# HGRN decays kept as factors and multiplied in place, level by level, and RWKV's normalisation taken by token halves

## The reference

```python
def rwkv7_time_mix(...):                       # B, its end: 8 heads of 64
    mean = jnp.mean(o, axis=-1, keepdims=True)
    var = jnp.mean(jnp.square(o - mean), axis=-1, keepdims=True)
    o = ((o - mean) * lax.rsqrt(var + RWKV_LN_EPS)).reshape(B, S, W_B)
    o = o * ln_w + ln_b
    o = o + bonus.reshape(B, S, W_B)
    return o * g

def hgrn2_mix(p, lower_bound, norm_w):         # C: 4 heads, 128 keys, 128 values
    q, fz, i, g = jnp.split(p, 4, axis=-1)
    q = jax.nn.silu(q).reshape(B, S, H_C, DK_C)
    log_f = jnp.logaddexp(jnp.log(lb), jnp.log1p(-lb) + jax.nn.log_sigmoid(fz))
    k = -jnp.expm1(log_f)                      # k = 1 - f
    o = hgrn2_chunked(q, k, i, log_f)          # S_t = f_t * S_(t-1) + k_t v_t ;  o_t = q_t S_t
    return rms_norm_2(o, norm_w) * jax.nn.silu(g)
```

## Time and profile before

| | us |
|---|---|
| median of 3 runs | 3694.24 (3691.92 to 3695.18) |
| the profiled execution | 3689.92 |
| its span | 3688.1 |
| PE busy | 3578.8 (97%) |
| DVE busy | 2229.6 (60%) |
| ACT busy | 1547.7 (42%) |

### The profile page before, as it was taken

One profiled execution on the slowest core, in us unless ns is written; L12 is line 12 of the kernel. 1 busy time (PEld: TensorE's weight loads), 2 busy tenths in 40 slices (PEclk: granted clock), 3 DMA queues, 4 the chain that ended last, 5 costly groups with the idle time before them and its releaser, 6 DMA issues.

```text
span 3688.1 us, 49956 instructions
## 1 busy us (share of the span) xinstructions
PE 3578.8 (97%) x19351; PEld 2892.5 (78%) x19351; DVE 2229.6 (60%) x2501; ACT 1547.7 (42%) x2051; POOL 1059.6 (29%) x567
## 2 busy tenths in 40 slices
PE   8999999999999999999999999998999999998999
PEld 7887888887888778888778786776788786776787
DVE  5666767567666357666666545547555545447654
ACT  4365444454344354444644432224444432324443
POOL 6800838404848018383057000011000001011000
PEclk9999999999999999999999999999999999998999
DMA  8745767556767257675466454312465553312563
GB/s 267 246 133 182 246 212 247 185 155 219 254 202 237 96 178 262 206 251 178 141 229 230 153 187 118 119 59 81 159 206 193 169 168 105 137 36 101 175 203 125
DMA packets 494426, 649.95 MB, mean 176 GB/s; under 512 B 17227, under 2 KB 394594, under 8 KB 494242
## 3 DMA queue, kind: packets, MB, share of 16 engines
q1 hardware_dynamic: 473508, 569.62, 46.8%
q0 software_dynamic: 19584, 75.50, 5.8%
q10 hardware_dynamic: 1150, 2.29, 0.2%
HBM read 646.29 MB, written 1.05 MB: 176 GB/s over the span
## 4 chain that ended last, share of the span: by engine, by line
issue 57%; POOLq 20%; PE 13%; POOL 7%; ACT 0%; DMA 0%; DVE 0%; SPq 0%; ACTq 0%; DVEq 0%
POOLq L642 8%; POOLq L644 6%; POOLq L646 6%; PE bank L1526 4%; PE bank L994 3%; POOL mod_zone L649 3%; POOL modrow L649 2%; PE bank L964 1%; POOL modrow L631 1%; POOL mod_zone L631 1%; PE bank L971 1%; PE bank L973 1%; PE bank L972 1%; POOL rstd L608 1%; PE bank L1723 0%
## 5 line engine op out<-in xcount | busy, mean ns | idle before, releaser
L2596 DVE TENSOR_TENSOR wproj_lo<-wproj,wproj_hi 128x2048 fp32r<-128x2048 f32 x252 | 757.4, 3010 | 129.4 <-ACT wproj_hi L1989 129.4
L994 PE MATMUL bank<-wproj_lo,x_hi 128*128 128x512 f32 x2112 | 538.4, 397 | 0.6 <-ACT x_hi L1980 0.6
L994 PE MATMUL bank<-wproj_hi,x_hi 128*128 128x512 f32 x2112 | 531.0, 393 | 6.6 <-DVE arena L2717 2.8
L994 PE MATMUL bank<-wproj_hi,x_lo 128*128 128x512 f32 x2112 | 523.6, 390 | 0.6 <-DVE x_lo L2657 0.6
L2038 ACT CAST actT_hi<-bank 128x512 fp32r<-128x512 f32 x132 | 77.5, 587 | 1051.1 <-PE bank L1022 1051.1
L994 PEld LDWEIGHTS bank<-wproj_hi,x_hi 128*128 128x128 f32 x2112 | 396.6, 189 | 96.9 <-issue 7.3
L1989 ACT CAST wproj_hi<-wproj 128x2048 fp32r<-128x2048 f32 x252 | 470.5, 1913 | 4.8 <-DMA wproj<-in_ffn_w_gate_up 4.6
L994 PEld LDWEIGHTS bank<-wproj_hi,x_lo 128*128 128x128 f32 x2112 | 396.6, 188 | 83.0 <-DVE x_lo L2657 1.1
L606 POOL TENSOR_SCALAR rstd<-sumsq 128x1 f32<-128x1 f32 x38 | 7.2, 190 | 1546.6 <-ACT tok L1961 1546.3
L994 PEld LDWEIGHTS bank<-wproj_lo,x_hi 128*128 128x128 f32 x2112 | 388.1, 189 | 79.3 <-ACT x_hi L1980 3.3
L2727 DVE TENSOR_TENSOR actT_lo<-bank,actT_hi 128x512 fp32r<-128x512 f32 x132 | 91.2, 691 | 566.0 <-ACT actT_hi L2038 566.0
(11 more groups left out here) (451 smaller groups left out, 5259.6 us busy)
## 6 DMA issues: line engine op xcount, KB each, us to landing
wproj<-in_ffn_w_gate_up SPq DMA_DIRECT2D x336, 512.0 KB, 6.2
wdown<-in_ffn_w_down SPq DMA_DIRECT2D x132, 1024.0 KB, 4.9
wproj<-in_ffn_w_gate SPq DMA_DIRECT2D x84, 512.0 KB, 5.0
wproj<-in_ffn_w_up SPq DMA_DIRECT2D x84, 512.0 KB, 6.2
wproj<-in_w_in SPq DMA_DIRECT2D x40, 1024.0 KB, 7.2
mod_zone<-in_mod_w POOLq DMA_DIRECT2D x36, 1024.0 KB, 6.4
modrow<-in_mod_w POOLq DMA_DIRECT2D x36, 1024.0 KB, 6.0
wproj<-in_sb_w_qkv SPq DMA_DIRECT2D x96, 256.0 KB, 4.3
```

Of the source, the lines that this page charges most:

```text
L994: last = nc.tensor.matmul(proj_ps[t][:, :], rounded(x_part[of_x](c)[:, toks]), rounded(w_part[of_w][:, c, :]), start=start and c == 0, sto ...
L2596: V.tensor_tensor(rounded(wproj_lo[w.odd][:, cols]), src[:, cols], wproj_hi[w.odd][:, cols], ALU.subtract).then_inc(cols_lo, 1)
```

## The change

**Factors for logarithms.** As soon as ACT has copied the first half of RWKV's outputs (`oc0`), it computes `hf` = sigmoid(fz), `hk` = sigmoid(-fz), `hq` = silu(q) and `h_g` = silu(g); `hgrn` on ACT no longer takes a part in the levels. DVE (`decays`) applies the lower bound in the second layer (two operations for each of 4 chunks, as before, but on the factors), and makes `decayed` = hq * hf. At each level DVE (`lengthen(m)`) multiplies the second halves of `decayed` by the product over their block's first half, and the first halves of `hk` by the product over the second, both in place, and makes the products of the next level in `h_total` (512, 256, ... 16 elements, none at m = 64). PE reads `hk` and `decayed` themselves. Since they are changed in place, DVE waits before each level until PE has finished the scores of the level before.

**RWKV's normalisation** up to `ln_ss` is done for each token half by itself, the first while ACT waits for the second. PE's `turn` moves from ahead of HGRN's first scores to behind values(1), and `finish_rwkv` is cut in three steps, one behind each of the levels 1, 2 and 3. ACT's casts (`xg_hi`, `o_hi`, blocks 1 and 2) are no longer spread over the levels but stand one behind the other.

The core of the diff:

```diff
 # PE, hgrn(l)
-                pe.wait_ge(*rw_v.at(l, "ln"))
-                turn(BC)
                 pe.wait_ge(*hg_in.at(l, "in"))
-                pe.wait_ge(*hg_upd.at(l, "upd"))
+                pe.wait_ge(*hg_keys.at(l, "keys"))
                 block_scores(0, hk, hq)
                 for i in range(n_lv):
-                    pe.wait_ge(*hg_x.at(l, "x", i))
-                    x = h_x[i % 2]
+                    pe.wait_ge(*hg_upd.at(l, "upd", i))
                     if i >= 3:
                         pe.wait_ge(*hg_acc.at(l, "acc", i - 3))
                     if i == 2:
                         pe.wait_ge(ln_ev, 2 * n.lin - 1)
                     if i < len(LEVELS) - 1:
-                        block_scores(i + 1, x, x)
+                        block_scores(i + 1, hk, decayed)
...
                     values(i)
+                    if i == 1:
+                        pe.wait_ge(*rw_v.at(l, "ln"))
+                        turn(BC)
 # ACT, rwkv(l)
                 for t in range(NT):
                     act.wait_ge(*rw_pe.at(l, f"o{t}"))
                     nc.scalar.copy(tok[:, t, 0:W_B], proj_ps[t][:, :]).then_inc(*rw_act.next(f"oc{t}"))
+                    if t == 0:
+                        nc.scalar.activation(hf.rearrange(flat), f_raw, ACT.Sigmoid)
+                        nc.scalar.activation(hk.rearrange(flat), f_raw, ACT.Sigmoid, scale=-1.0).then_inc(*hg_f.next("f"))
+                        nc.scalar.activation(hq.rearrange(flat), q_raw, ACT.Silu).then_inc(*hg_in.next("in"))
+                        nc.scalar.activation(h_g.rearrange("p t n -> p (t n)"), g_raw, ACT.Silu).then_inc(*hg_g.next("g"))
 # ACT, hgrn(l)
-                for i, m in enumerate(LEVELS + [P]):
-                    act.wait_ge(*hg_upd.at(l, "upd", i))
-                    if i >= 1:
-                        act.wait_ge(*hg_x.at(l, "x", i - 1))
-                    e, f, g = (halves(x, m) for x in (h_e, hf, hs))
-                    nc.scalar.activation(e[:, :, 1], f[:, :, 1], ACT.Exp)
-                    nc.scalar.activation(e[:, :, 0], g[:, :, 0], ACT.Exp).then_inc(*hg_ex.next("ex"))
...
+                copy_odd(BC, lambda c: vec[:, 1 + l, w + c:w + c + 1],
+                         lambda c: vec[:, 1 + l, b_at + c:b_at + c + 1], oT[1])
+                round_block(l, 1)
+                act.wait_ge(*rw_v.at(l, "out"))
+                nc.scalar.copy(rounded(o_hi[1][:]), oT[1][:]).then_inc(*parts_hi.next("o1"))
+                round_block(l, 2)
 # DVE
             def decays(l):
...
+                v.wait_ge(*hg_f.at(l, "f"))
                 if l > 0:
...
+                        V.tensor_scalar(hf[:, c], hf[:, c], lows[:, 5, c:c + 1], lows[:, 4, c:c + 1], ALU.mult, ALU.add)
+                        V.tensor_scalar(hk[:, c], hk[:, c], lows[:, 5, c:c + 1], None, ALU.mult)
...
+                v.sem_inc(*hg_keys.next("keys"))
+                v.wait_ge(*hg_in.at(l, "in"))
+                V.tensor_tensor(decayed, hq, hf, ALU.mult).then_inc(*hg_upd.next("upd"))
+
+            def lengthen(m):
...
+                V.tensor_tensor(queries[:, :, 1], queries[:, :, 1], total[:, :, 0:1].broadcast_to(shape), ALU.mult)
+                V.tensor_tensor(keys[:, :, 0], keys[:, :, 0], total[:, :, 1:2].broadcast_to(shape),
+                                ALU.mult).then_inc(*hg_upd.next("upd"))
+                if m < BLK:
+                    to = BC * SEQ - BC * SEQ // m
+                    V.tensor_tensor(h_total[:, to:to + g], total[:, :, 0], total[:, :, 1], ALU.mult)
...
+                take(0)
+                for i, m in enumerate(LEVELS):
+                    v.wait_ge(*hg_s.at(l, "s", i + 1))
+                    v.drain()
+                    lengthen(m)
+                    take(i + 1)
+                    if 1 <= i <= 3:
+                        finish_rwkv(l, i - 1)
                 take(n_lv)
```

More of the change, by code:

```diff
@@ L411, in program @@
         place[0] = 0
-        hq, hk, hf, hs = (view(BC, SEQ) for _ in range(4))
-        h_t, h_e = view(BC, SEQ), view(BC, SEQ)
-        h_x = [view(BC, SEQ) for _ in range(2)]
+        h_total = view(BC * SEQ)
+        h_g = view(NT, W_C)
+        hf = view(BC, SEQ)
+        place[0] = 2 * 4 * P * 4 + 4 * 2 * 4 * BLK
+        decayed, hq = view(BC, SEQ), view(BC, SEQ)
         h_part = [view(8, BLK) for _ in range(2)]
         h_cross = view(4, P)
-        h_g = view(NT, W_C)
+        place[0] = 9 * BC * SEQ + 3 * SEQ
+        hk = view(BC, SEQ)
         h_v = modrow[:, 2, :].rearrange("p (t n) -> p t n", t=NT)
@@ new lines, in hgrn @@
+                for t in range(NT):
+                    act.wait_ge(proj_done, 2 * n.load + 1 + t)
+                    nc.scalar.copy(first_gate[:, t, :], (down_ps[3], proj_ps[0])[t][:, :]).then_inc(ln_ev, 1)
+                for half in range(2):
+                    chunks = slice(half * BC, (half + 1) * BC)
+                    nc.scalar.copy(rounded(xg_hi[:, chunks, :]), xT[:, chunks, :]).then_inc(*parts_hi.next("x"))
+                nc.scalar.copy(rounded(o_hi[0][:]), oT[0][:]).then_inc(*parts_hi.next("o0"))
@@ L2534, in bounds @@
                 act.wait_ge(low_d, 2)
[L2535 removed]
+                nc.scalar.activation(lows[:, 4:6], lows[:, 0:2], ACT.Exp).then_inc(low_s, 1)
             def squares(gain=None):
@@ L3266, in rwkv @@
[L3266 to L3274, removed]
@@ L3275, in rwkv @@
-                V.tensor_reduce(stats[0], sq, AX.X, ALU.add).then_inc(*rw_v.next("ln_ss"))
-                decays(l)
+                decays(l)
+                o, sq = (tok[:, :, k * W_B:(k + 1) * W_B].rearrange("p t (h d) -> p t h d", d=N_B) for k in range(2))
+                sums, rs = [x.rearrange("p (t h) -> p t h", t=NT) for x in (ln_ss[:, :], ln_rs[:, :])]
+                for t in range(NT):
+                    v.wait_ge(*rw_act.at(l, f"oc{t}"))
+                    V.tensor_reduce(sums[:, t], o[:, t], AX.X, ALU.add)
+                    v.drain()
+                    V.tensor_scalar(sums[:, t], sums[:, t], 1.0 / N_B, None, ALU.mult)
+                    v.drain()
+                    V.tensor_tensor(o[:, t], o[:, t], sums[:, t].unsqueeze(2).broadcast_to([P, H_B, N_B]), ALU.subtract)
+                    v.drain()
+                    V.tensor_tensor(sq[:, t], o[:, t], o[:, t], ALU.mult)
+                    v.drain()
+                    last = V.tensor_reduce(sums[:, t], sq[:, t], AX.X, ALU.add)
@@ L3277, in rwkv, with finish_rwkv @@
+                last.then_inc(*rw_v.next("ln_ss"))
                 v.wait_ge(*rw_pool.at(l, "ln_rs"))
-                V.tensor_tensor(o, o, stats[1].unsqueeze(3).broadcast_to([P, NT, H_B, N_B]), ALU.mult)\
+                V.tensor_tensor(o, o, rs.unsqueeze(3).broadcast_to([P, NT, H_B, N_B]), ALU.mult)\
                     .then_inc(*rw_v.next("ln"))
-            def finish_rwkv(l):
+            def finish_rwkv(l, step):
                 def scalars(name, c):
@@ L3285, in scalars @@
                     return vec[:, 1 + l, at:at + 1]
[L3287 to L3291, removed]
-                                .rearrange("p (c s) -> p c s", c=BC), ALU.add)
-                v.drain()
-                V.tensor_tensor(oT[1][:], oT[1][:], oT[2][:], ALU.mult).then_inc(*rw_v.next("out"))
-                v.drain()
+                if step == 0:
+                    v.wait_ge(*hg_g.at(l, "g"))
+                    copy_even(BC, lambda c: scalars("ln_w", c), lambda c: scalars("ln_b", c), oT[1])
+                elif step == 1:
+                    v.wait_ge(ev_odd, n.odd)
+                    v.drain()
+                    V.tensor_tensor(oT[1][:], oT[1][:], gate[:].rearrange("p t n -> p (t n)")
+                                    .rearrange("p (c s) -> p c s", c=BC), ALU.add)
+                else:
+                    v.drain()
+                    V.tensor_tensor(oT[1][:], oT[1][:], oT[2][:], ALU.mult).then_inc(*rw_v.next("out"))
             def rest_of_block(l, b, halves=range(2)):
@@ L3311, in hgrn @@
                 n.gates = n.load
-                if l > 0:
-                    v.wait_ge(*hb_ln.at(0, "ln"))
-                    V.scalar_tensor_tensor(hf, hf, 0.0, h_t, ALU.max, ALU.add)
-                    v.drain()
-                    for c in range(BC):
-                        V.tensor_scalar(hf[:, c], hf[:, c], lows[:, 0, c:c + 1], None, ALU.add)
-                v.drain()
-                v.sem_inc(*hg_upd.next("upd"))
                 def take(i):
```

91 lines of the change are left out of this document (16 added, 75 removed).

## The result

The changed kernel takes 3663.52 us (median of 4 runs, 3660.17 to 3665.44) against 3694.06 (4 runs, 3691.92 to 3695.18): ratio 0.9918, 95% interval 0.9906 to 0.9931, so 30.5 us less. 3670.7 was forecast, with a range from 3665.0 to 3679.0.

What follows compares the result with a forecast made beforehand. PE, 97% busy, was held by waits for RWKV's normalisation and for DVE and ACT at HGRN's levels. 26.8 us saved at full clock less 3.3 for half clock, 23.5, gave 3666.4; plus 4.3 for a median, 3670.7, range 3665.0 to 3679.0.

Steps and rivals of the forecast that it cites:

- A to B: From the gate block's end (A) to HGRN's last matmul (B): 42.67 and 47.66 us, forecast savings 12.2 and 14.6.
- the DVE and ACT circle: At each HGRN level PE waits for DVE and ACT: 3.87 us a level, against PE's own 3.00.
- rival 3: Gain given back behind B as blocks 3 and on wait for loads; saves 14 to 19 us, 3678; chance 0.05.
- From T to B: PE's remaining levels and transposes, 25.1 us, plus 0.7 of waits at levels with `finish_rwkv`: 25.8 at full clock.
- the slack: At each level DVE's in-place work, 1.4 us, fits under PE's values, 1.91, so it costs nothing.
- T: End of DVE's `take(0)`, for which PE waits: A + 4.7 us in layer 0, A + 7.3 in layer 1.
- From there to the last multiply took 5.30: From RWKV's sums of squares to the multiply by POOL's result: 5.30 us, taken over from the old trace.
- the lower bound: Layer 1, DVE ahead of `take(0)`: 8 operations more, 0.27 us apart, so 2.1 to 2.3 us.
- The clock: Half clock after PE's waits of 2.5 and 5.1 us: loses 2.2 in layer 1, 1.1 in layer 0 (even odds).
- the full-clock case: Full clock from T on in both layers: saves 26.8 us, 3667.4; chance 0.12.
- Rival 4: PE to DVE to PE circle holds half clock through all levels: B at T + 45.5, 3707 us; chance 0.03.

Runs made afterwards that it cites:

- Experiment 6: Changed kernel plus one more DVE multiplication of 512 elements ahead of each lengthening; A to B 31.09 and 34.59 us in layers 0 and 1.
- Experiment 7: Changed kernel plus a DVE memset and a two-input DVE operation, writing spare space, under POOL's power; A to B 32.16 and 35.48 us.
- experiment 3: Changed kernel with only the transposes put back ahead of HGRN's first scores; A to B 29.79 and 34.72 us.
- experiment 4: Changed kernel with RWKV's normalisation put back to one piece, transposes still behind values(1); A to B 29.93 and 31.79 us.
- experiment 5: Kernel before with only the transposes moved behind values(1), ACT's copy one level later; median 3698.24 us against 3691.91, ratio 1.0019.
- experiment 9: Changed kernel plus only the two-input DVE operation, writing spare space, under POOL's power; A to B 29.16 and 33.06 us.
- experiment 8: Changed kernel plus only the DVE memset, writing spare space, under POOL's power; A to B 28.25 and 32.33 us.
- experiment 10: Changed kernel with DVE's first level put ahead of its multiply by POOL's result; median 3655.78 us against 3661.96 for the change, 3691.91 before.

## Why the prediction was right in kind and short in size

**The bound.** Right: time lay in A to B, in waits for the normalisation and for the DVE and ACT circle. Nothing was given back behind B (rival 3): from B to the first branch matmul pass 1.17 or 1.18 us in both kernels, and the medians gained 30.5, no less than A to B with 29.3.

**From T to B.** Forecast 25.8 at full clock; measured 25.5 in layer 0 (T 2514.76, B 2540.27). The waits in it are 0.39 and about 0.15, where 0.7 was forecast. Experiment 6 shows the slack that I had worked out. Right.

**T.** This is the step that failed, in the prediction's words "From there to the last multiply took 5.30". I took the time from the sums of squares to the multiply over from the earlier trace rows as POOL's latency. It is POOL's latency with DVE's old `decays` beside it. The change moves `decays` away, and the latency is 3.37. So T was A + 2.75 where A + 4.7 stood, and A + 5.7 in layer 1 where A + 7.3 stood: 2.0 and 1.6 us. In layer 0 that is the whole miss: the sums of squares ended at A - 2.56, as forecast. In layer 1 two misses partly cancel. The latency was taken 2.3 too long (the 5.30 and the "little longer"), and the lower bound 0.7 too short: from its first operation to the next product passed 2.90, where 2.1 to 2.3 stood. I had even written that `decays` lay under POOL's power, and had looked at it only as work that POOL hides, not as work that slows POOL. Experiment 7 puts the load back and gets 67.6 for the sum, a saving of 22.7 us; 23.5 was forecast. Its T is A + 4.7 and A + 7.2. With the old latency the forecast would have held.

**The clock.** I took 2.2 us in layer 1 and 1.1 in layer 0; 1.6 and 0 were lost. That term hangs on the same step: PE's wait in layer 0 is 0.79, not 2.5. Ahead of the levels, waits of 2.08 and 2.46 (experiments 3 and 4, layer 0) brought no fall, and those of 2.71, 2.81 and longer did. The length of the wait doesn't decide it alone: in layer 1 of the kernel before, PE waited 2.08 at 3342.4 at full clock, ran scores in 1.15, waited 0.82, and the values behind were at half. What else decides it stays open. The forecast had no more than even odds for layer 0.

```profile
3344.46 1.15 PE L1857 MATMUL bank<-arena 128*64 128x64 f32 x32 [2.08 <-DVE arena L3343]
```

**The sum.** T came 3.6 us earlier than forecast, 1.7 too much was taken for the clock, and T to B is 0.5 shorter: 23.5 + 5.8 = 29.3. The medians gained 1.2 more than that, which I can't place and which lies inside the interval. The range's low end, 3665, was the full-clock case plus a little; it had no bound for the one latency that was taken over as it stood. The nearest rows for it were POOL's own two operations, and the first of them behind B, which took 1.11 in place of 2.13.

**The rivals.** Rival 4 (half clock through all levels, 3707) did not happen: clock 1.00 and 0.95 in A to B. The Trainium skill, "TensorE: Matmul & The Clock Gate", section "A second HAM failure mode: psum-queue depth-cycling", tells of a clock that swings under short idle times between groups of matmuls. The traces here don't agree for these levels: with waits of up to 0.40, and of 1.05 and 1.35 in layer 0 of experiment 6, the granted clock stayed 1.00. That the old kernel with the transposes moved was slower (experiment 5) is a way of becoming slower that I had not seen.

## What to carry to other kernels

A wait taken over from the old trace holds only with the neighbours it had: before using a latency of POOL, look at what DVE did in the same microseconds and whether the change moves it (here 5.30 became 3.37). When a producer's place is moved back, look at what consumes it in program order: the consumer's engine must have something else to give in the meantime, else the stall returns larger, and with a clock penalty. Compare stretches between two events of the same engine, not spans, where runs differ by more upstream than the term in question.

## What the hardware showed that I had not expected

A tensor-scalar of POOL on 128x16 elements takes 0.21 us alone, 0.21 beside a DVE memset, 1.11 beside a DVE operation of two SBUF inputs that had begun 0.17 us earlier, and 2.13 where such an operation stands second behind the memset. In the last two cases it ends 0.06 and 0.07 us after the two-input operation. For the first of them (experiment 9):

```profile
2508.01 1.11 POOL L680 TENSOR_SCALAR ln_rs<-ln_ss 128x16 f32<-128x16 f32 x1 [36.27 <-DVE ln_ss L3264]
```

```profile
2507.84 1.22 DVE L3266 SCALAR_TENSOR_TENSOR arena<-lora_w,arena 128x1024 f32<-128x1024 f32 x1
```

The Trainium skill, "SBUF — State Buffer", section "Who interferes with whom", says that a DVE instruction with two SBUF inputs contends with a GpSimd instruction that reads SBUF and that the one to issue first keeps the ports; the row with 1.11 agrees. The case of 2.13 goes further: POOL's operation starts at 2508.82, when DVE's two-input one is not yet running (2509.72), and would have been over at 2509.03; it still ends behind it. Why, the runs do not show. Nor does every DVE operation with two SBUF inputs lengthen every one of POOL: the power took 2.90 us in both layers of the changed kernel and of experiments 7 to 10, also beside the lengthening of experiment 10. It took 3.23 beside the lower bound's operations in layer 1 of the kernel before, and 3.68 in HGRN's normalisation of every kernel.
